# Layer 0 and 1 of a hybrid decoder step: output product and first norm laid out by features instead of by tokens

## What is computed

```python
for i in range(DEPTH):
    ...
    y = jnp.einsum('bsc,cd->bsd', gb * conv, w_out)        # layer 1: gelu(gate) * h
    ...
    xp = layer_norm(ALPHA * xp + yp, ln1_g[i], ln1_b[i])
    mp = hier_moe(xp, moe_w_group[i], moe_w_expert[i], moe_w_gate[i], moe_w_up[i], moe_w_down[i])
    xp = layer_norm(ALPHA * xp + mp, ln2_g[i], ln2_b[i])
```

## Time and profile before

| | us |
|---|---|
| three timed runs | 1622.78, 1628.49, 1630.34 (median 1628.49) |
| profiled execution, its own time | 1624.22 |
| its span in the trace | 1622.5 |
| TensorE busy | 1315.3 (81%) |
| VectorE, ScalarE, GpSimd busy | 367.5, 172.1, 114.8 |
| mean granted TensorE clock | 0.936 of full speed |
| moved by the DMA engines | 490.78 MB, 302 GB/s over the span |

### The profile page before, as it was taken

How to read it: one execution, slowest core, us unless ns; L and a number is a source line. 1 busy time by engine, 2 the same in 40 slices (tenths; PEclk the granted TensorE clock), 3 DMA queues, 4 the chain that set the end, 5 groups by cost and what they waited for, 6 DMA issues and landing times.

```text
span 1622.5 us, 19205 instructions
## 1 busy us (share of the span) xinstructions
PE 1315.3 (81%) x7984; PEld 851.9 (53%) x7984; DVE 367.5 (23%) x707; ACT 172.1 (11%) x265; POOL 114.8 (7%) x120
## 2 busy tenths in 40 slices
PE   8999997899878787878259998979987778787750
PEld 7888744566444444444148873556654444444420
DVE  1211133311101010101265664341111010100017
ACT  1000000000000000000014552010000000000000
POOL 0000010100000000000220000110000000000003
PEclk9999998899999999999769999979999999999985
DMA  9932424799999999999759115369999999999965
GB/s 240 363 134 104 138 62 120 275 401 395 413 405 413 403 412 408 416 406 423 230 153 353 58 47 179 94 216 392 409 403 410 404 412 395 415 399 409 418 227 147
DMA packets 118683, 490.78 MB, mean 302 GB/s; under 512 B 13648, under 2 KB 48464, under 8 KB 102249
## 3 DMA queue, kind: packets, MB, share of 16 engines
q1 hardware_dynamic: 92010, 434.03, 68.4%
q10 hardware_dynamic: 19654, 39.11, 8.0%
q0 software_dynamic: 6976, 17.05, 3.9%
HBM read 468.86 MB, written 25.45 MB: 305 GB/s over the span
## 4 chain that ended last, share of the span: by engine, by line
PE 44%; DMA 24%; SPq 22%; DVE 4%; issue 3%; POOL 2%; ACT 1%; ACTq 0%; DVEq 0%; POOLq 0%
SPq L357 22%; PE ps L524 17%; PE ps L737 10%; DMA ring<-in_moe_w_up 8%; DMA ring<-in_moe_w_gate 7%; PE ps L611 7%; PE ps L756 5%; DMA ring<-in_moe_w_down 4%; DMA Bt<-yrows,slot_i 2%; PE ps L727 1%; DMA ring<-in_a_w_in 1%; POOL stat L462 1%; PE ps L630 1%; PE ps L537 1%; PE ps L670 1%
## 5 line engine op out<-in xcount | busy, mean ns | idle before, releaser
L737 PE MATMUL ps<-ring,A 128*64 128x256 f32 x4096 | 488.3, 394 | 115.1 <-DMA ring<-in_moe_w_up 85.1
L737 PEld LDWEIGHTS ps<-ring,A 128*64 128x64 f32 x4096 | 322.7, 142 | 300.4 <-issue 117.8
L524 PE MATMUL ps<-A,ring 128*128 128x260 f32 x1280 | 286.5, 386 | 5.6 <-DMA ring<-in_a_w_in 3.7
L756 PE MATMUL ps<-ring,C 128*64 128x512 f32 x1024 | 236.5, 603 | 51.3 <-DMA ring<-in_moe_w_down 18.6
L524 PEld LDWEIGHTS ps<-A,ring 128*128 128x128 f32 x1280 | 245.3, 192 | 44.4 <-issue 3.9
L1347 DVE TENSOR_TENSOR C<-C,ps 128x256 f32<-128x256 f32 x64 | 26.9, 420 | 849.3 <-ACT C L1001 849.3
L756 PEld LDWEIGHTS ps<-ring,C 128*64 128x64 f32 x1024 | 78.3, 138 | 168.5 <-issue 144.9
L611 PE MATMUL ps<-ring,Bt 128*104 128x512 f32 x320 | 140.7, 597 | 0.0
L475 POOL DMA_INDIRECT A<-x,idx x64 | 59.3, 927 | 840.8 <-PE ps L727 785.0
L611 PEld LDWEIGHTS ps<-ring,Bt 128*104 128x104 f32 x320 | 54.3, 172 | 78.4 <-issue 78.1
L1001 ACT ACTIVATE C<-ps 128x256 f32<-128x256 f32 x64 | 24.5, 383 | 577.1 <-PE ps L737 577.1
(11 more groups left out here) (170 smaller groups left out, 558.4 us busy)
## 6 DMA issues: line engine op xcount, KB each, us to landing
ring<-in_moe_w_gate SPq DMA_DIRECT2D x64, 2048.0 KB, 39.4
ring<-in_moe_w_up SPq DMA_DIRECT2D x64, 2048.0 KB, 32.9
ring<-in_moe_w_down SPq DMA_DIRECT2D x64, 2048.0 KB, 36.7
ring<-in_a_w_in SPq DMA_DIRECT2D x24, 512.0 KB, 8.0
yrows<-C ACTq DMA_DIRECT2D x88, 96.0 KB, 6.3
ring<-in_b_w_in SPq DMA_DIRECT2D x8, 1024.0 KB, 11.6
C<-x ACTq DMA_DIRECT2D x15, 416.0 KB
x<-C ACTq DMA_DIRECT2D x13, 416.0 KB
```

Source lines behind the costliest of these rows:

```text
L524: mm = pe.matmul(bank, lhs(k), rhs(k), start=(k == 0), stop=(k == KT - 1))
L737: mm = pe.matmul(ps[hf * ROWS:(hf + 1) * ROWS, 1, u * FH:(u + 1) * FH], xgT[:, k, :], ring[:, slot, col:col + FH], start=(k == 0), stop=(k ...
L756: mm = pe.matmul(ps[nh * ROWS:(nh + 1) * ROWS, 2, :], hidT[:, at:at + ROWS], ring[:, slot, m * D + nh * 512:m * D + (nh + 1) * 512], start ...
```

## The change

The output product keeps a block of weights (128 columns, 8 elements apart) in the array and streams a half of `hT`: its result lies by features, in 8 blocks `m` of two halves. VectorE adds the residual from `xT`, where it still is, and writes the sum back to `xT`. ScalarE squares each block and VectorE adds the squares up. TensorE takes the logits of the norm's raw input with router weights that carry the norm's scale, the sums over features with a column of ones, and the sums of squares with one more matmul for each tile. VectorE corrects the logits with mean and deviation. Then TensorE turns the tiles back to tokens, ScalarE normalizes them on the way out of PSUM into `xk` (L942), without the norm's scale and bias, and they are written to `x1_dram`. The scale and bias are applied where the rows are turned again: `turned_rows` of each expert becomes a multiply and an add.

`xk` stays on chip as the residual of the second norm. Its scale and bias are applied on VectorE during experts 1 and 2. Nothing is loaded as a residual any more, and `x2_dram` is gone. ScalarE's queue loads the norms' parameters after expert 0, in layer 1 again after expert 2. In the second norm ScalarE takes the sum of squares (`spread`), in layer 0 it also normalizes (`normal`), and the turned tiles are copied into `xT` by VectorE and ScalarE with scale and bias. SyncE's wait for the x2 writes is gone. At the start, three of five input tiles go ahead of the first weights on SyncE's queue, all five are turned before the first product, and there are 12 instead of 24 warming matmuls.

The diff, cut to its core; in the parts on TensorE's loop, on ScalarE and on VectorE the removed lines are not shown, since they are the old code printed above:

```diff
+FIRST_BANK = (0, 2, 4, 6, 0)
+FIRST_ORDER = (0, 2, 1, 3, 4)
 WARM = 12
+PAIR = (0, 1, 2, 3, 0, 1, 2, 0)
...
+        xk = [C[:TT, i * D:(i + 1) * D] for i in range(NT)]
...
+        gain, shift = Bt[:TT, 0:D], Bt[:TT, D:2 * D]
+        picks = [[[v[:TT, (2 * i + k) * D:(2 * i + k + 1) * D] for k in range(TOPK)] for i in range(2)]
+                 for v in (Bt, A)]
...
-                        if m == 2:
-                            all_out(sp, 1)
...
-                    out = ring[:, ring_slot(pos), :].rearrange("p (k n) -> p k n", k=KT)
-                    sp.dma_start(out, w_out[l][:, :, u * 512:(u + 1) * 512]).then_inc(loaded[ring_slot(pos)], 16)
+                    out = ring[:, ring_slot(pos), :].rearrange("p (k n) -> p k n", k=KT // 2)
+                    sp.dma_start(out, w_out[l][:, u * KT // 2:(u + 1) * KT // 2, :]).then_inc(loaded[ring_slot(pos)], 16)
...
-                for i in range(NT):
-                    root(2 * l, i)
...
+                pool.wait_ge(var_ok, l + 1 + l * NT)
+                pool.tensor_tensor(stat[:, 3, :], stat[:, 2, :], half_neg[:, :], ALU.pow).then_inc(rstd_ok, 1)
+                pool.wait_ge(x1_out, 16 * NT * (l + 1))
+                pool.wait_ge(turned1, NT * (l + 1))
...
-                q = 2 * l + 1
+                pool.wait_ge(scaled, l + 1)
                 for i in range(NT + 1):
                     if i < NT:
                         if i >= 2:
-                            pool.wait_ge(z_done, NT * q + i - 1)
...
+                            pool.wait_ge(sq2_ok, NT * l + i - 1)
+                        for k in range(TOPK):
                             c = k * NT + i
                             pool.indirect_dma_start(
-                                out=r, out_offset=None, in_=rows_dram,
+                                out=picks[l][i % 2][k], out_offset=None, in_=rows_dram,
                                 in_offset=bass.IndirectOffsetOnAxis(ap=slot_i[:, c:c + 1], axis=0),
                             ).then_inc(pick_in[2 * l + i % 2], 16)
                     if i >= 1:
-                        root(q, i - 1)
+                        pool.wait_ge(var_ok, (l + 1) + l * NT + i)
+                        pool.tensor_tensor(stat[:, 3, i - 1:i], stat[:, 2, i - 1:i], half_neg[:, :1],
+                                           ALU.pow).then_inc(rstd_ok, 1)
...
-            def out_part(l, i, lo, hi, first=False):
...
+            def out_part(l, m, lo, hi, free=False):
+                for hf in range(2):
                     for k in range(lo, hi):
-                        mm = pe.matmul(ps[:TT, 2 * (i % 2) + nh, :], hT[:, k, i * TT:(i + 1) * TT],
-                                       ring[:, s, k * 512:(k + 1) * 512], start=(k == 0), stop=(k == KT - 1))
-                        if first and nh == 0 and k == lo:
+                        s = ring_slot(POS_OUT[l] + k // (KT // 2))
+                        col = (k % (KT // 2)) * D + m
+                        mm = pe.matmul(ps[:, 2 * PAIR[m] + hf, :HALF], ring[:, s, col:col + D - KT + 1:KT],
+                                       hT[:, k, hf * HALF:(hf + 1) * HALF], start=(k == 0), stop=(k == KT - 1))
+                        if free and hf == 0 and k == lo:
                             mm.then_inc(freed, 1)
-                    ends.append(mm)
-                return ends
+                return mm
...
+                    out_part(l, 1, 0, EARLY, free=True)
+                    pe.wait_ge(sig_ok, 2 * KT)
+                    out_part(l, 2, 0, EARLY)
+                    out_part(l, 3, 0, EARLY)
+                pe.wait_ge(h_done[l], KT)
+                for m in range(KT):
+                    if m >= 4:
+                        pe.wait_ge(zT_done, KT * l + m - 3 if m < KT - 1 else KT * l + 5)
+                    out_part(l, m, EARLY if m < (1, 4)[l] else 0, KT).then_inc(out_mm, 1)
+                    if m == 4:
+                        state_rows()
+                pe.wait_ge(st_sb, l + 1)
+                pe.wait_ge(wg_ok, l + 1)
+                for k in range(KT):
+                    mm = pe.matmul(ps[:TT, 6, 200:200 + NC], wr[:, k, NC:].broadcast_to([P, TT]), wr[:, k, :NC],
+                                   start=(k == 0), stop=(k == KT - 1))
+                    if k == 0:
+                        mm.then_inc(freed, 2)
...
+                for i in range(NT):
                     for k in range(KT):
+                        if i == 0:
+                            pe.wait_ge(zT_done, KT * l + k + 1)
+                        pe.matmul(ps[:TT, 6, i * (NC + 1):(i + 1) * (NC + 1)], xT[:, k, i * TT:(i + 1) * TT],
+                                  wr[:, k, :], start=(k == 0), stop=(k == KT - 1))
+                pe.wait_ge(zsum_ok, KT * (l + 1))
                 for i in range(NT):
+                    mm = pe.matmul(ps[:TT, 6, 300 + i:301 + i], sq_sum[:, i * TT:(i + 1) * TT], wr[:, 0, NC:],
+                                   start=True, stop=True)
+                mm.then_inc(logit_mm, 1)
+                for i in range(NT):
+                    turn_token(i)
...
-                def project(u, slot, free):
+                def project(u, slot, free, prior=True):
                     for k in range(KT):
                         for hf in range(2):
...
                             mm = pe.matmul(ps[hf * ROWS:(hf + 1) * ROWS, 1, u * FH:(u + 1) * FH],
                                            xgT[:, k, :], ring[:, slot, col:col + FH],
                                            start=(k == 0), stop=(k == KT - 1))
-                            if free and (k, hf) in ((0, 0), (KT - 1, 1)):
+                            if free and (k, hf) in (((0, 0),) * prior + ((KT - 1, 1),)):
...
+                def square(m):
+                    act.wait_ge(zT_done, KT * l + m + 1)
+                    if m >= 2:
+                        act.wait_ge(zsum_ok, KT * l + m)
+                    act.activation(sq if m else sq_sum, xT[:, m, :], ACT.Square).then_inc(zsq_ok, 1)
...
+                act.wait_ge(norm_ok, l + 1 + l * NT)
                 for i in range(NT):
+                    act.wait_ge(turned1, NT * l + i + 1)
+                    act.activation(xk[i].rearrange("r (p k) -> r k p", k=KT),
+                                   ps[:TT, 2 * (i % 3):2 * (i % 3) + 2, :].rearrange("r a (k p) -> r (a k) p", k=4),
+                                   ACT.Identity, bias=stat[:, 4, i:i + 1], scale=stat[:, 3, i:i + 1]).then_inc(xn_done, 1)
+                    act.wait_ge(xn_done, 2 * NT * l + i + 1)
+                    act.dma_start(x1_dram[l][i * TT:(i + 1) * TT, :], xk[i]).then_inc(x1_out, 16)
...
+                    if e == 0:
+                        act.wait_ge(idx_ok[l], 2)
+                        norm_loads(2 * l)
+                        if l == 0:
+                            router_weights(1)
+                    if e == 2 and l == 1:
+                        act.wait_ge(scaled, l + 1)
+                        norm_loads(2 * l + 1)
...
+                def spread(i):
+                    act.wait_ge(mean_ok, NT * l + i + 1)
+                    act.activation(picks[l][i % 2][0], xk[i], ACT.Square, bias=stat[:, 5, i:i + 1], scale=1.0 / 32,
+                                   accum_out=stat[:, 6, i:i + 1]).then_inc(sq2_ok, 1)
...
+                for m in range(KT):
+                    dve.wait_ge(out_mm, KT * l + m + 1)
+                    stt(halves(xT[:, m, :]), halves(xT[:, m, :]), ALPHA, banks(PAIR[m]), ALU.mult, ALU.add).then_inc(zT_done, 1)
...
+                    else:
+                        add_square(m - 1)
+                add_square(KT - 1)
...
+                raw = ps[:TT, 6, :NT * (NC + 1)].rearrange("p (i c) -> p i c", i=NT)
+                step(tsc(stat[:, 0, :], raw[:, :, NC], 1.0 / D, ALU.mult))
...
+                step(tt(lgm, by_token(stat[:, 0, :]), by_logit(0), ALU.mult))
+                step(tt(lg, raw[:, :, :NC], lgm, ALU.subtract))
+                dve.wait_ge(rstd_ok, l + 1 + l * NT)
+                stt(stat[:, 4, :], stat[:, 0, :], -1.0, stat[:, 3, :], ALU.mult, ALU.mult).then_inc(norm_ok, 1)
+                step(tt(lg, lg, by_token(stat[:, 3, :]), ALU.mult))
+                step(tt(lg, lg, by_logit(1), ALU.add))
...
-                def turned_rows(done, ready, v):
+                def turned_rows(done, half, ready, v):
                     dve.wait_ge(done, v)
-                    dve.tensor_copy(xgT, ps[:, 0, :KT * ROWS].rearrange("p (k t) -> p k t", k=KT)).then_inc(ready, 1)
+                    tt(xgT, ps[:, 0, :KT * ROWS].rearrange("p (k t) -> p k t", k=KT),
+                       gb[:, 2 * l, :].unsqueeze(2).broadcast_to([P, KT, ROWS]), ALU.mult).then_inc(half, 1)
+                    dve.wait_ge(half, v)
+                    tt(xgT, xgT, gb[:, 2 * l + 1, :].unsqueeze(2).broadcast_to([P, KT, ROWS]), ALU.add).then_inc(ready, 1)
...
+                    if e == 1:
+                        dve.wait_ge(par_in, 32 * (l + 1))
```

(40 more changed lines are left out.)

403 lines of the change are left out of this document (170 added, 233 removed).

## The result

The changed kernel takes 1668.92 us, median of 4 runs (1665.21 to 1673.38), against 1629.41 of 4 runs of the kernel before on the same chip (1622.78 to 1632.66): ratio 1.0249, 95% interval 1.0225 to 1.0273. It is 40 us slower; forecast was 1611, 15 us faster. The profiled execution has a span of 1671.6 us against 1622.5, 49.1 more.

The account below looks back on a forecast made before the run. DMA bounds the expert loops, the engines' path the stretches between. Start -1, first norms -17.3 and -22.9, loops +7.5, layer 0's second norm +15.6, end +3.0 sum to -15.1: 1626.5 becomes 1611 us, range 1594 to 1630.

Parts of the forecast that it names:

- the chain: First norm, from the last logits to the first expert's product: 22.1 us in each layer.
- 122 records at 1.57/16 = 0.098: The 61 small matmuls behind the output product (constants, logits, squares) take 0.098 us a record, 12.0 us in all.
- rival (c): Gathers slowed about 5 us more per landing, or small matmuls at cold pace 0.19: 1626, no change; chance 0.18.
- I charge nothing: Output product: loading stationary weight columns 32 bytes apart hides under the 0.215 us of a matmul, so no cost.
- rival (d): Strided weights set the output product's pace; from 0.244 a record the whole gain is gone: 1626 to 1691; chance 0.06.
- Five passes of 1.1: ScalarE's first-norm normalization passes take 1.1 us each, hidden beside the chain to the index table with some 2 us slack.
- The loops, +3.0 and +4.5: Expert loops of layers 0 and 1: new parameter loads cost 4.0 and 5.5 us, less 1 us gain in each.
- Layer 0's second norm, +15.6: Layer 0's second norm gets longer: 5.6 us from serialized gathers, 10 from weights loading beside them; bounds 5 to 31.
- The ring: Second norms: landing, addition, variance, root and next gather issue run in series, 3.4 us plus one landing per tile from the third.
- Rival (e): Layer 0's second norm under a full DMA throughout, landings of 14 us each: 1632 and more; chance 0.04.
- Layer 1's product and first norm, -22.9: Layer 1's output product to its first expert gets 22.9 us shorter; bounds 18 to 25.
- The end, +3.0: Layer 1's second norm, first addition to last write: 42.7 us against 39.7, with landings of 7.0; bounds 0 to 9.

Follow-up runs that it names:

- e6_contig: Changed kernel with the output product's 128 stationary weight columns taken in a row, not every eighth; values not the reference's: 1696.7 us, ratio 1.0440.
- e3_read: Changed kernel with ScalarE's first-norm normalization pass reading PSUM by stride and writing x in order: 1661.0 us, ratio 1.0202.
- e10_best: Changed kernel with all repairs: variance order, SyncE's wait, early router weights, strided PSUM read, later residual scaling and second gain/shift, more warming: 1621.3 us, ratio 0.9961.
- e11_rows: e10_best with gain and shift loaded as one row each and spread by TensorE into PSUM: 1605.9 us, ratio 0.9860.
- e5_hold: Changed kernel with SyncE holding layer 1's third input-weight block until layer 0's second norm has squared its last tile: 1654.4 us, ratio 1.0158.
- e1_order: Changed kernel with VectorE's variance step of tile i-1 issued ahead of tile i's first addition in both second norms: 1653.9 us, ratio 1.0151.
- e2_router: Changed kernel with layer 1's router weights loaded ahead of layer 0's normalization passes, not behind expert 0: 1668.8 us, ratio 1.0244.
- e12_warm: Changed kernel with four more warming products between the turn of the first expert's rows and its first product: 1671.2 us, ratio 1.0268.

## Why the prediction was wrong

The mechanisms were mostly named; one was not (ScalarE's blocked queue), two stood only in rivals (the strided weights, the small matmuls at a low clock), and nearly each size was set at its low end.

- **To layer 0's first expert, -18.3, measured -3.1.** Four terms share the 15.2: the start (-1, measured +1.5), the product's pace (0.215 a record and 56.0 in all, measured 0.240 and 62.2), the small matmuls (0.098 and 12.0, measured 15.4) and the chain (22.1, measured 25.2). 2.5 + 6.2 + 3.4 + 3.1.
- **"122 records at 1.57/16 = 0.098"** failed: this pace was read from a group of 16 that stood between products of 512 columns, and carried to 122 small records in a row. The constants kept it; the logits began at it and then fell to a granted clock of 0.50, in both layers of the changed kernel and of every kernel made from it. So the second half of rival (c), small matmuls at the cold pace, came true in part, 3.4 us in layer 0 and 5.6 in layer 1, and the argument against it (a cold row stands behind an idle TensorE) does not hold: TensorE had been busy without a gap. No run tried to keep the clock up there.
- **"I charge nothing" for the strided weights** failed: it was argued from short loads with an average of 0.12. The load did become the pace, though only just: rival (d)'s point of 0.244, where the product's whole gain is gone, was nearly met. e6_contig gives 0.020 of the 0.025 back; the rest is not explained. The Trainium skill (SBUF — State Buffer, "Door 1: The DMA port swizzle") has it that an access that crosses to another 16-byte line pays a penalty, as elements 32 bytes apart do each time; by that rule the trace agrees, 336 against 190 ns.
- **"Five passes of 1.1"** failed, and "beyond that each us costs one" held: 2.2 us each made ScalarE the last of the chain. e3_read shows the stride of the write as the cause: with 1.2 us a pass the chain took 22.4.
- **The loops, +3.0 and +4.5, measured +13.5 and +12.3.** Three things are behind it. Gain and shift were costed by an idle stretch, 3.6 us of engine time; 8 rows instead of 104 gave back 7 in each loop, VectorE's wait for them included. "VectorE's scaling fits beside experts 1 and 2" was wrong: it waits 8.3 us for their landing in layer 1. And ScalarE's queue, 17 us in the issue of one expert's writes of rows, stood in no part of the prediction. The last two cost little alone, since the next late engine takes their place; e10_best, free of all of them at the head, still has 492.9 and, less its late last expert, 493.1. e11_rows leaves 3.4 us of the excess in loop 0 (491.2) and none in loop 1 (488.2); what the 3.4 are stays open. The first expert's low clock delays the first free slot by 2 to 3 us, which was not foreseen either.
- **Layer 0's second norm, +15.6, measured +24.6** (from the last result to the input product's main run: 844.32 - 784.35 = 60.0 before, and 84.6 now, with 3.6 for the 16 records of the early product that stand in the row at 875.84). The ring was right in its structure, and in its size to the tenth, the latter by luck: e5_hold, which has it without the weights, takes 50.3 us from the first addition (805.61 to 852.26 + 3.6), where the prediction had 50.2. Its landings were 6.8 to 6.9 and not 6.5 (whose own terms, 2.8 and 3.5, add up to 6.3), so the last addition came at 34.0 instead of 32.5, and the steps behind it took 16.3 instead of 17.7. The contention was put at 10 and measured 18.9: 3.4 in the first landing and 15.5 behind it. It was inside the bounds (0 and 25), at its far side. Rival (e)'s landings of 14 us were met by one pair of four. The Trainium skill (DMA: Bandwidth & Descriptors, "Queues, rings and completion order") lets a DMA engine take turns between its queues by the packet; half the pace for a pair beside a busy queue is an estimate from that rule, by which the landings would be some 3.5 longer. They were 5.3 and 7.7 longer than the 6.9 and 6.8 of e5_hold, so the direction agrees and the size does not.
- **Layer 1's product and first norm, -22.9, measured -8.5.** (1077.66 - 983.26 = 94.4 before, 1103.87 - 1017.95 = 85.9 now.) From the mixer's last step (1017.95) to the product's end it took 42.8 against 37.4, the small matmuls 17.6 against 12.0, the chain 25.5 against 22.1: the same three terms as in layer 0.
- **The end, +3.0, measured +9.2** from first addition to last write: the landing was 8.5 to 9.0, not 7.0, at the upper bound. GpSimd's first issue of a pair took 1.7 there and 1.0 in layer 0. The order alone makes it: e1_order gives 8.4 of the end's 10.6 us back.

The range failed since errors were taken to cancel. All seven terms came out worse than their value, and five of them (both first norms, both loops, the end) worse than their worse bound.

## What to carry to other kernels

A step that waits on nothing itself still delays what is queued behind it: put an engine's short step for tile i-1 ahead of its wait for tile i, which gave 8 and 14 us here for one moved line. Loads that look small by their bytes are to be priced with what waits for them: 104 copies of two rows, 2.1 us by bytes, cost 7 us in a loop whose VectorE waited for them and 6 ahead of its last expert; with two rows and four matmuls instead, the loops were back to within 3.4 us of the kernel before. A pace read from a short group between long matmuls is not the pace of a long row of short ones: 0.098 became 0.136 and 0.163 when the clock fell. A stride of 32 bytes in SBUF was better taken as one of 512 bytes in PSUM: a pass of 2.2 us became 1.2, with the same values.

## What the runs showed of the hardware that was not expected

- 128 stationary columns 32 bytes apart load in 336 ns, in a row in 190; with 260 columns moving this makes 0.240 us a record against 0.220.
- ScalarE's 104x1024 pass takes 2.20 us with a write every 32 bytes in SBUF and 1.20 with a read every 512 bytes in PSUM.
- A DMA's issue on ScalarE's queue, mostly 0.4 us, took 8.8 us for router weights in small pieces, and the next two together, the writes of rows, 17.1, while the engine did nothing else. With the router weights loaded elsewhere (e2_router) these two took 0.81.
- A gap of 1.58 us ahead of the first expert's product was followed by a granted clock of 0.66 and 0.50 in the next 5 us (layers 0 and 1), one of 0.85 by 1.00 in both the earlier trace rows. With the gap filled to 0.49 it was 1.00 in layer 0 and 0.76 in layer 1, where TensorE had stood 3.49 us ahead of the turn (e12_warm); 1.00 in both layers of e10_best; and 0.79 and 1.00 in e11_rows. 0.50 is 1.2 GHz, 1.00 is 2.4.
- In a row of 122 matmul records of 36, 37 and 1 columns, with TensorE never idle, the granted clock fell from 1.00 to 0.50 during the 80 of 37 columns: 25 records in 2 us before, 14 after. These 80 took 10.8 to 13.8 us in layer 0 and 11.1 to 13.8 in layer 1.
- A pair of gathers (0.85 MB) lands in 6.9 us with no weight loads beside it (a share of 0.35 with its own) and in 12.2 to 14.5 at a share of 1.03.
